# Attention scores from (low, high) queries against doubled high keys, with the compressed mask folded into constant rows

## What is computed

```python
q = apply_rope(q, cos, sin)                      # (1024 tokens, 8 heads, 64)
kc = compress_blocks(k_c, ...)                   # 63 blocks of 32 tokens, stride 16
sc = einsum('bsghd,bngd->bghsn', q, kc) * scale  # compressed branch
valid = (arange(nc) * 16 + 31)[None, :] <= arange(s_len)[:, None]
p = softmax(where(valid, sc, -1e30)) * valid
# selected and window branches: the same with full keys, causal and a band of 512
```

## Time and profile before

| | |
|---|---|
| median of 3 runs | 943.73 us |
| the profiled execution: its time, its span | 942.87 us, 941.0 us |
| TensorE busy, share of the span | 896.5 us, 95% |
| VectorE, ScalarE, GpSimd busy | 521.6, 394.5, 213.9 us |
| share of TensorE in the chain that ended last | 86% |
| granted TensorE clock, mean | 0.998 |
| first score of head 0, of head 7 | at 322.64 us, 569.34 us |

### The profile page before, as it was taken

How to read it: one execution, slowest core, us unless ns; L and a number is a source line. 1 busy time by engine, 2 the same in 40 slices (tenths; PEclk the granted TensorE clock), 3 DMA queues, 4 the chain that set the end, 5 groups by cost and what they waited for, 6 DMA issues and landing times.

```text
span 941.0 us, 14439 instructions
## 1 busy us (share of the span) xinstructions
PE 896.5 (95%) x5585; PEld 738.8 (79%) x5593; DVE 521.6 (55%) x1090; ACT 394.5 (42%) x793; POOL 213.9 (23%) x213
## 2 busy tenths in 40 slices
PE   2799999999999999999999999999999999999997
PEld 2478999689999877777777776788888888877885
DVE  3652284368765397797797796732222122246454
ACT  6642232522123368768768768731111111132221
POOL 3369812101100103203203212255650000000000
PEclk9999999999999999999999999999999999999999
DMA  9946042041010000000000001233231121133222
GB/s 299 338 158 90 7 113 68 1 94 45 1 46 1 1 1 1 1 1 1 1 2 1 1 1 35 76 104 106 62 107 50 46 52 38 66 128 120 89 90 90
DMA packets 61156, 59.69 MB, mean 63 GB/s; under 512 B 10240, under 2 KB 53824, under 8 KB 61072
## 3 DMA queue, kind: packets, MB, share of 16 engines
q1 hardware_dynamic: 58832, 54.13, 19.9%
q0 software_dynamic: 2000, 4.54, 1.8%
q10 hardware_dynamic: 256, 0.09, 0.0%
HBM read 52.92 MB, written 5.24 MB: 62 GB/s over the span
## 4 chain that ended last, share of the span: by engine, by line
PE 86%; DVE 5%; ACT 4%; DMA 2%; POOL 1%; issue 1%; SPq 0%; DVEq 0%; another core or an unknown queue 0%; POOLq 0%; ACTq 0%
PE bank L1715 40%; PE win_max L1715 23%; PE slc_max L1715 19%; PE bank L1718 4%; DMA xs<-in_x 1%; DVE rt L1205 1%; POOL cld L648 1%; DVE mx L1517 1%; ACT phi L845 1%; ACT q L845 1%; DMA cld<-in_c_im 1%; DVE mx L1524 1%; ACT pt L845 0%; ACT osb L845 0%; ACT yt L845 0%
## 5 line engine op out<-in xcount | busy, mean ns | idle before, releaser
L1205 DVE TENSOR_TENSOR plo<-pt,phi 128x512 fp32r<-128x512 f32 x192 | 110.2, 590 | 40.7 <-ACT phi L845 40.2
L845 ACT ACTIVATE pt<-bank 128x512 f32<-128x512 f32 (+1 forms) x208 | 100.2, 482 | 63.7 <-PE bank L1715 60.7
L1715 PE MATMUL bank<-q,k 128*128 128x512 f32 (+7 forms) x384 | 102.1, 347 | 0.1
L845 ACT ACTIVATE phi<-bank 128x512 fp32r<-128x512 f32 (+1 forms) x208 | 100.1, 481 | 0.0
L630 POOL TENSOR_TENSOR qa<-qa,otmp 128x256 f32<-128x256 f32 x32 | 26.3, 822 | 201.8 <-DVE otmp L1205 201.8
L1715 PEld LDWEIGHTS bank<-q,k 128*128 128x128 f32 (+1 forms) x384 | 62.6, 190 | 10.9 <-ACT phi L845 2.7
L1517 DVE TENSOR_REDUCE mx<-slc_max 128x1 f32<-128x128 f32 (+3 forms) x64 | 48.2, 753 | 11.0 <-PE slc_max L1715 9.0
L1715 PE MATMUL bank<-ht_hi,dhi 128*128 128x512 f32 x128 | 49.8, 389 | 0.0
L1715 PE MATMUL bank<-ht_lo,dhi 128*128 128x512 f32 x128 | 49.8, 389 | 0.0
L1715 PE MATMUL bank<-ht_hi,dlo 128*128 128x512 f32 x128 | 49.8, 389 | 0.0
L1205 DVE TENSOR_TENSOR dtm<-bank,dsig 128x512 f32<-128x512 f32 x16 | 11.1, 692 | 68.2 <-ACT dsig L845 68.2
(11 more groups left out here) (440 smaller groups left out, 2590.1 us busy)
## 6 DMA issues: line engine op xcount, KB each, us to landing
ada<-in_w_ada SPq DMA_DIRECT2D x16, 512.0 KB, 10.4
draw<-in_w_in SPq DMA_DIRECT2D x16, 512.0 KB, 3.9
wraw<-in_w_in SPq DMA_DIRECT2D x7, 1024.0 KB, 6.6
xs<-in_x SPq DMA_DIRECT2D x8, 512.0 KB, 8.5
gstage<-in_w_ada POOLq DMA_DIRECT2D x16, 256.0 KB, 3.0
oraw<-in_w_out SPq DMA_DIRECT2D x8, 512.0 KB, 6.6
xr<-in_x SPq DMA_DIRECT2D x8, 512.0 KB, 4.2
out<-yr SPq DMA_DIRECT2D x7, 512.0 KB, 2.9
```

Source lines behind the costliest of these rows:

```text
L845: return nc.scalar.activation(o, i, fn, **kw)
L1205: return V.tensor_tensor(o, a, b, op)
L1715: return T.matmul(o, l, r, start=start, stop=stop, **kw)
```

## The change

The two matmuls of a score tile share the work in another way. The first is (low, high) query x (high, high) key: `q1` now holds the low query above the high one, `k1` the high key twice. The second is (constant rows, high) query x (constant rows, low) key: rows 64 to 127 of `q2` hold the high query again, `k2` the low key; rows 0 to 5 hold the maxima as before, and rows 6 and up a table of steps that, times a matching table in `k2c` (now one for each half of the queries), gives the compressed mask. The bf16 mask matmul of the compressed branch is gone.

What feeds them changes with it:
- GpSimd's second copy of the high query (`PQ` on GpSimd) is gone; `PL` writes its low part into `qc1`, and `MQ` waits for it.
- `PL` of head h+2 stands at unit 23 of head h; in the opening, `PL` of head 1 stands behind the first pair of maxima.
- ScalarE has new copies: `QC`, rows 64 to 127 of `q1` into `q2`, 1024 wide, at unit 6 of each head for the next; `QA`, the table of steps into `q2`, once for each of the two buffers (opening, and unit 4 of head 0).
- `MM` is now four matmuls with a six-column weight (`qaug`) and the fp32r identity `identr`, in place of four fp32 transposes.
- `key_high` is two copies of 64 rows in place of one of 128, and `key_rows` waits for both.
- `compressed_keys_values` has another list of small instructions.

The diff, cut to its core (left out: constants placed elsewhere in SBUF, removed waits on GpSimd's copy, the wait of `MC` on `MM`, the copies of `identr` and `cmpt` on VectorE):

```diff
-        aug[HD + 2 * b:HD + 2 * b + 2, b] = 1.0
+        aug[2 * b:2 * b + 2, b] = 1.0
+    seen = np.clip((np.arange(SEQ) - CMP_STRIDE + 1) // CMP_STRIDE, 0, NCMP)
+    steps = np.zeros((HD, SEQ + 2 * 64), f32)
+    steps[0:2, SEQ:] = 1.0
+    for c in range(NC_HALF):
+        first_seen = seen[HALF * c]
+        for m in range(HALF // CMP_STRIDE + 1):
+            steps[6 + m, HALF * c:HALF * c + HALF] = seen[HALF * c:HALF * c + HALF] == first_seen + m
+            steps[6 + m, SEQ + 64 * c:SEQ + 64 * c + 64] = np.where(np.arange(64) < first_seen + m, 0.0, MASK)
     return {"t_rope": rope, "t_ident": ident, "t_masks": np.concatenate([causal, band], 1),
-            "t_cmpq": cmp_q, "t_cmpt": np.concatenate([cmp_q.T, cmp_q.T], 0), "t_ramp": ramp, "t_aug": aug}
+            "t_cmpq": cmp_q, "t_cmpt": steps, "t_ramp": ramp, "t_aug": aug}
...
-            ("MQ", 0, 1), ("PQ", 1)]
+            ("MQ", 0, 1), ("PQ", 1), ("QA", 0), ("QC", 0)]
     for i in range(ST):
         plan += pair(i) + [("Z", 2 + i // 2, 4 * (i % 2), 4 * (i % 2) + 4)]
+        if i == 0:
+            plan.append(("PL", 1))
     plan += [("MC", 0, p) for p in range(4)]
-    plan += [("Z", 6, 0, KT), ("MM", 0, 0), ("Z", 7, 0, KT), ("MM", 0, 1), ("PL", 1)]
+    plan += [("Z", 6, 0, KT), ("MM", 0, 0), ("Z", 7, 0, KT), ("MM", 0, 1)]
...
-        if more and u == 2 and h >= 1:
-            plan.append(("PL", h + 1))
+        if e == 4:
+            plan.append(("QA", 1))
+        if more and u == 6:
+            plan.append(("QC", h + 1))
...
+        if more and u == 23 and h + 2 < HEADS:
+            plan.append(("PL", h + 2))
...
+    identr = const("identr", [P, P], R)
...
-    cmpt = const("cmpt", [P, SEQ], B, 2)
+    cmpt = const("cmpt", [P, SEQ + 2 * 64], B, 2)
...
-    NQ2 = HD + 6
-    qc2 = at("qc2", [P, ST, NQ2], F, R_W + 34304)
+    NAUG = 6
+    qaug = at("qaug", [P, ST, NAUG], R, R_W + 34304)
...
-                nc.gpsimd.tensor_copy(k2[b][HD:P, :, :],
-                                      aug[HD:P, b + 1:b + 2].unsqueeze(1).to_broadcast([HD, GROUPS, SEQ]))\
+                nc.gpsimd.tensor_copy(k2[b][0:HD, :, :],
+                                      aug[0:HD, b + 1:b + 2].unsqueeze(1).to_broadcast([HD, GROUPS, SEQ]))\
...
-                if step[0] == "PQ":
-                    if n_low:
-                        pool.wait_ge(once("plo_cmp"), n_low)
-                    if n_sum:
-                        pool.wait_ge(once("norm"), n_sum)
-                    n_dup += 1
-                    pool.wait_ge(once("qhi"), step[1] + 1)
-                    nc.gpsimd.tensor_copy(qc1[:, :, 1, :], f(qc1[:, :, 0, :])).then_inc(once("qdup"), 1)
-                elif step[0] == "S" and units[step[1] % NU][0] == 0:
...
-                a(k1[b][:, :, P * i:P * i + P], bk[:, 0:2 * P].rearrange("p (g s) -> p g s", g=GROUPS))\
+                a(k1[b][0:HD, :, P * i:P * i + P], bk[0:HD, 0:2 * P].rearrange("p (g s) -> p g s", g=GROUPS))\
                     .then_inc(once("k1"), 1)
+                a(k2[b][HD:P, :, P * i:P * i + P], bk[HD:P, 0:2 * P].rearrange("p (g s) -> p g s", g=GROUPS))\
+                    .then_inc(once("k1"), 1)
...
-                    a(qc1[:, :, 0, :], v, scale=1.0 / math.sqrt(HD)).then_inc(once("qhi"), 1)
+                    a(qc1[:, :, 1, :], v, scale=1.0 / math.sqrt(HD)).then_inc(once("qhi"), 1)
+                elif step[0] == "QA":
+                    if step[1] == 1:
+                        act.wait_ge(s_unit, len(unit_list))
+                    n_q2 += 1
+                    a(q2[step[1]][0:HD, :], cmpt[0:HD, 0:SEQ]).then_inc(once("q2"), 1)
+                elif step[0] == "QC":
+                    h = step[1]
+                    if h == 0:
+                        act.wait_ge(s_trf, first["q"] + 2)
+                    else:
+                        act.wait_ge(once("b7"), b7_after[("MQ", h, 1)])
+                    n_q2 += 1
+                    a(q2[h % 2][HD:P, :], f(q1[h % 2][HD:P, :])).then_inc(once("q2"), 1)
...
-                    a(q2[h % 2][0:NQ2, hf * HALF:(hf + 1) * HALF], bank[7][0:NQ2, :]).then_inc(once("b7"), 1)
+                    act.wait_ge(once("q2"), n_q2)
+                    a(q2[h % 2][0:NAUG, hf * HALF:(hf + 1) * HALF], bank[7][0:NAUG, :]).then_inc(once("b7"), 1)
...
-                ch.mark(V.memset(f(k1c[:, :, :]), 0.0))
-                ch.link(V.memset(f(k2c[:, :, :]), 0.0))
+                ch.mark(V.memset(f(k1c[:, :, :, :]), 0.0))
+                ch.link(V.memset(f(k2c[HD:P, :, :, :, :]), 0.0))
                 dve.wait_ge(once("kcps"), 1)
                 kp = bank[2][:, 2:2 + GROUPS * NCMP]
                 kp3 = kp.rearrange("p (g n) -> p g n", g=GROUPS)
+                for c in range(NC_HALF):
+                    ch.mark(V.tensor_copy(k2c[0:HD, c, :, :, :].rearrange("p g a n -> p (g a) n"),
+                                          cmpt[0:HD, SEQ + 64 * c:SEQ + 64 * c + 64].unsqueeze(1)
+                                          .to_broadcast([HD, 2 * GROUPS, 64])))
                 for a_ in range(2):
-                    ch.mark(V.tensor_copy(k1c[0:HD, :, a_, 0:NCMP], kp3[0:HD]))
-                    ch.mark(V.tensor_copy(k2c[0:HD, :, a_, 0:NCMP], kp3[0:HD]))
-                ch.link(V.tensor_copy(kch[HD:P, :], kp[HD:P]))
-                for a_ in range(2):
-                    ch.mark(tt(k1c[HD:P, :, a_, 0:NCMP], kp3[HD:P],
-                               f(kch[HD:P, :]).rearrange("p (g n) -> p g n", g=GROUPS), ALU.subtract))
-                    ch.mark(V.tensor_copy(k2c[HD:P, :, a_, :],
-                                          aug[HD:P, 0:1].unsqueeze(1).to_broadcast([HD, GROUPS, 64])))
+                    ch.mark(V.tensor_copy(k1c[:, :, a_, 0:NCMP], kp3))
+                ch.wait()
+                for c in range(NC_HALF):
+                    for a_ in range(2):
+                        ch.mark(tt(k2c[HD:P, c, :, a_, 0:NCMP], kp3[HD:P], f(k1c[HD:P, :, a_, 0:NCMP]), ALU.subtract))
...
-                    if h >= 1:
-                        dve.wait_ge(once("mt"), 2 * h)
                     v = qa[:, h // 2, :, HD * (h % 2):HD * (h % 2) + HD]
-                    V.scalar_tensor_tensor(out=qc2[:, :, 0:HD], in0=v, scalar=1.0 / math.sqrt(HD),
-                                           in1=f(qc1[:, :, 0, :]), op0=ALU.mult, op1=ALU.subtract)\
+                    V.scalar_tensor_tensor(out=qc1[:, :, 0, :], in0=v, scalar=1.0 / math.sqrt(HD),
+                                           in1=f(qc1[:, :, 1, :]), op0=ALU.mult, op1=ALU.subtract)\
...
-                dve.wait_ge(once("k1"), m + 1)
-                V.tensor_copy(k2[b][0:HD, :, P * i:P * i + P],
+                dve.wait_ge(once("k1"), 2 * m + 2)
+                V.tensor_copy(k1[b][HD:P, :, P * i:P * i + P],
...
-                    pe.wait_ge(once("qdup"), h + 1)
+                    pe.wait_ge(once("qhi"), h + 1)
+                    pe.wait_ge(once("qlo"), h + 1)
...
-                    pe.wait_ge(once("qlo"), h + 1)
...
-                        ins = tr(bank[7][0:NQ2, P * q:P * q + P], qc2[:, 4 * hf + q, :])
+                        ins = mm(bank[7][0:NAUG, P * q:P * q + P], qaug[:, 4 * hf + q, :], identr[:, :], True, True)
...
-                    ins = mm(o, K2(br, g, ks), q2[h % 2][0:NQ2, lo:hi_], False, not (dg or bd or br == 0))
-                    if br == 0:
-                        ins = mm(o, identb[:, :], cmpt[:, lo:hi_], False, True)
```

More of the change, by code:

```diff
@@ L773, in _ @@
                 ch.link(nc.gpsimd.memset(f(vhi[b][:, :, :, HD:VW]), 1.0))
[L774 to L775 removed]
+                nc.gpsimd.tensor_copy(k2[b][0:HD, :, :],
+                                      aug[0:HD, b + 1:b + 2].unsqueeze(1).to_broadcast([HD, GROUPS, SEQ]))\
                     .then_inc(once("k2aug"), 1)
                 pool.wait_ge(once("k2aug"), b + 1)
[L781 to L791 removed]
+            n_low = n_sum = 0
+            for step in plan:
+                if step[0] == "S" and units[step[1] % NU][0] == 0:
                     e = step[1]
[L794 removed]
                     if n_low:
@@ L807, in _ @@
                     pool.wait_ge(once("b7"), b7_after[step])
-                    pool.wait_ge(once("qdup"), n_dup)
                     pool.wait_ge(once("plo_cmp"), n_low)
@@ L1295, in _ @@
             V.tensor_copy(identb[:, :], ident[:, :]).then_inc(once("identb"), 1)
+            V.tensor_copy(identr[:, :], ident[:, :]).then_inc(once("identb"), 1)
             dve.wait_ge(once("den"), 1)
@@ L1537, in attention_step @@
                         dve.wait_ge(once("mneghi"), h + 1)
+                        if h >= 1:
+                            dve.wait_ge(once("mt"), 2 * h)
                         V.tensor_copy(q2v[:, :, :, 0], f(mneg_hi[:, :, :])).then_inc(once("mcat"), 1)
@@ L2002, in _ @@
             K1 = lambda br, g, s: k1c[:, g, :, :].rearrange("p a n -> p (a n)") if br == 0 else k1[br - 1][:, g, s]
-            K2 = lambda br, g, s: (k2c[:, g, :, :].rearrange("p a n -> p (a n)") if br == 0 else k2[br - 1][:, g, s])[0:NQ2]
```

(4 more changed lines are left out.)

37 lines of the change are left out of this document (18 added, 19 removed).

## The result

The changed kernel takes 950.34 us (median of 4 runs, 949.73 to 951.83); the kernel before, on the same chip, 944.24. The ratio is 1.0068, with a 95% interval of 1.0049 to 1.0088: slower by 0.7%, outside the range of the forecast. The profiled execution took 951.83 us, its span is 950.0 against 941.0. These 9.0 us are more than the 6.1 between the medians, since the profiled execution is the slowest of the four, and that of the kernel before was one of its quickest.

The account below looks back on a forecast made before the run. TensorE was taken to set the time in the heads, VectorE's chain at the key transposes. Key stage +0.5, opening +1.3 - 0.2, head 0 +0.5, passages -1.7, QC +1.4, passage 6 to 7 -0.4: +1.4, giving 945.1 us, range 941.2 to 949.0.

Parts of the forecast that it names:

- Opening, "+1.3 (0.9 to 1.6)": Before head 0, MQ waits for PL, which stands behind later key copies: MQ at 296.65 instead of 295.36, +1.3 us.
- The clock falls in the opening: Rival: TensorE's 1.3 us longer idle time brings 1.2 GHz, adding 2 to 3 us of work: 947.6; chance 0.05.
- Key stage, +0.5 (0 to 1.0): Before the heads, an extra ScalarE copy to wait for and a wider clearing delay VectorE and TensorE's key transposes: +0.5 us.
- Head 0, +0.5: QA and QC copies within three units of head 0, partly covered by ScalarE's gaps: +0.5 us, bounds 0 and 1.9.
- The opening's MM term, -0.2: The two MM in the opening, as matmuls instead of fp32 transposes, give -0.2 us at best.
- QC, +0.23: ScalarE's new copy between exponentials of units 6 and 7 delays osb of unit 8: +0.23 us in each of six heads.
- The slower rival: QC is exposed whole, 0.95 instead of 0.23 us per head, since ScalarE sets the pace there: 950.8; chance 0.18.
- Passages, 0.29 of 0.67: Where heads meet, 0.29 of up to 0.67 us saved arrives, VectorE and GpSimd holding each other: -1.7 us over six.
- the 0.08 of the pair: The matmul pair behind MM takes 0.71 us after transposes, another 0.63; the 0.08 should go with the transposes.
- MM at unit 21 "gains nothing": TensorE's next transposes already wait 0.21 us for ScalarE's copy of that MM, so an earlier MM gains nothing.
- third rival: QC is exposed whole on ScalarE between unit 6 and osb, 5.7 us more than forecast: 950.8; chance 0.18.

Follow-up runs that it names:

- early key copies: Changed kernel with ScalarE making the two key copies of tile m-2 before, not behind, the high part (kcat) of tile m: 947.31 us, ratio 1.0042 to the kernel before.
- late gates: Changed kernel with ScalarE's gate sigmoid and table load behind the q1 copies, first silu behind the last key copies: 945.06 us, 1.0008 to the kernel before.
- both mendings of the opening: Changed kernel with key copies ahead of kcat and gate sigmoid behind the q1 copies, heads as in the changed kernel: 944.06 us, 0.9998 to the kernel before.

## Why the prediction was wrong, point by point

- **Opening, "+1.3 (0.9 to 1.6)": the step that failed.** From the fourth key transposes to MQ the changed kernel takes 3.65 us more, where I had 1.3: 2.8 is the wait for PL, as named, but of another size (2.91 where TensorE had idled 0.1), and 0.8 comes at the last key transposes. I put the key copies where they stand in the earlier trace rows and added half a microsecond. I did not follow VectorE's wait for the second copy through the tiles in which it has a backlog (+1.75 at the query copy), nor see that the two table loads would now stand within MQ's chain. The runs with early key copies (-2.0), with late gates (-2.6) and with both (-3.75) show it, and with both the whole loss is gone.
- **"The clock falls in the opening", a rival at 0.05: it came about.** The profile has three stretches at 1.2 GHz outside the end: near 205 (1.5 us), behind MQ's wait (2.1) and in head 0 (1.3; 1.1 to 1.4 in the four profiles that have one there), 5 of the 9.0 us. The one behind MQ comes from the change, shown by the filled wait. The first is no part of the change: the kernel before has the same idle time, its profile with the mask matmul doubled has the stretch too, and the run with it filled suggests that most of its slower executions come from there. The one in head 0 comes beside a wait for ScalarE's copy into `q1`, 1.79 us here and 1.56 in the kernel before; whether the longer wait brings it is not shown. My remark that idle times near 1 us left the clock at 1.00 was true, but the wait is 2.9 us, not the 1.3 of my sum.
- **Key stage, +0.5 (0 to 1.0).** The wait grew from 0.99 to 1.81: +0.8. Within its bounds.
- **Head 0, +0.5.** +0.65 where the clock is undisturbed (36.35 against 35.70). Moving QC took off 0.37, moving QA 0.4. Right. The opening's MM term, -0.2, was not measured alone; the stretch of work that holds both MM, from the second window maximum to the first score, takes 0.25 less.
- **QC, +0.23.** 0.3, and at another place, the score of unit 9. Size near, place wrong. The slower rival, that QC is exposed whole (0.95), gave 950.8, half a microsecond from the measured time, by a mechanism that doesn't happen. The agreement is chance.
- **Passages, 0.29 of 0.67.** The hold between VectorE and GpSimd is there and agrees with the Trainium skill, SBUF — State Buffer, on who interferes with whom: the low part of 384 columns takes 1.10 us behind PL and beside the addition, 0.55 in the run with PL at unit 21. But it cost 0.08 per head, not 0.38. A late value product is not a late score: the matmuls behind it have slack of their own. The lead that the masks bring is 0.38 after the first seven microseconds of a head. MM at unit 25 gives 0.11; the 0.08 of the pair behind it is void. So some 0.49 arrives.
- **MM at unit 21 "gains nothing".** Right, and it was worse than that: the 0.21 of the earlier trace rows grew to 0.45, and ate 0.24 of TensorE's lead from wherever it came. I used that row for MM alone and not for the masks and all else that comes before it in the head. PQ at unit 16 shows it: 0.32 per head.
- In sum the heads 1 to 6 gave -0.9 where I had -0.7: errors that nearly cancel, too little gain in the passage, and too little loss at QC and none at unit 22. That this part came out near is luck.
- Without the stretches near 205 us and in head 0 the measured terms are: key stage +0.8, from there to MQ +3.65, clock behind MQ +2.1, the rest of the opening -0.25, head 0 +0.65, heads 1 to 6 -0.9, behind them -0.2. That is 5.85, near the 6.1 between the medians; I had 1.4, and the opening alone accounts for the difference.
- **The range.** Its upper end of 949.0 leaves out not the upper half of the third rival, as I wrote, but its centre (950.8) as well.

## What to carry to other kernels

When a step gets a new input, write down the whole chain ahead of that input on its engine, table loads and in-order neighbours included, and not only the length of the new edge. An engine with a backlog turns each new short wait into a shift of everything behind it. And a wait of TensorE's that is a few tenths long tells that a second engine sets the time there: a gain of TensorE's before that place stops at it, until work is taken out of the other engine's full stretch.

## What the runs showed of the hardware

- TensorE's idle time of 2.0 us near 203 us was followed by a stretch at 1.2 GHz in 8 of the 14 profiles in which it stands, of variants of both kernels, and in none of the three in which it is filled. It cost 1.5 us.
- 2.9 us of idle time ahead of MQ was followed by one in all four profiles that have it, for 3.4 to 10.2 us, and it cost 1.5 to 3.7 us; 1.75 us there was not, in the one profile there is. 1.8 us in head 0 was, in 4 of 14 profiles of the changed kernel and its variants; 1.3 to 1.6 us there, in three of the kernel before and its variants, was not.
- Matmuls that nobody reads, put into such an idle time, made a kernel faster: 8 transposes took 1.06 us instead of 1.94.
- Filling one idle time does not end it: in two of the four filled kernels' profiles the low clock was in head 0. How the chip picks the place is open; the profile with both mendings of the opening has one near 34 us.
- The low part of 128x384 took 1.10 us beside GpSimd's addition and 0.55 without it, but the period changed by only 0.08.
- Also open is a lag that all other profiles have on that of the kernel before long before the first changed step that TensorE waits for: 0.2 to 1.2 us at the table load near 198. The two variants of the kernel before have it too (0.4), so it is not the change alone that brings it.
